# Two attention-and-FFN blocks on one core: all weight slots 192 bytes above the split activations, modulo 256

## What is computed

```python
def first_block(x, ...):
    for i in range(2):
        h = rmsnorm(x, norm_g[i])
        y = fox_mixer(h, ...) if i % 2 == 0 else nsa_mixer(h, ...)
        x = x + y
    return rmsnorm(x, final_g)

def second_block(x, ...):
    for layer in range(2):
        h = _rmsnorm(x, norm_mix[layer])
        y = _hgrn2_mixer(h, ...) if layer % 2 == 0 else _mla_mixer(h, ...)
        x = x + y
        x = x + _conv_ffn(_rmsnorm(x, norm_ffn[layer]), ...)   # 1024 -> 2 x 2816 -> 1024
    return x
```

## Time and profile before

| | |
|---|---|
| median of 3 runs | 1044.48 us (1043.44 to 1045.8) |
| profiled execution | 1047.28 us, its span 1045.5 us |
| TensorE (PE) busy | 1015.4 us, 97% |
| weight loads (PEld) busy | 967.8 us, 93% |
| VectorE (DVE) busy | 767.1 us, 73% |
| ScalarE (ACT) busy | 549.9 us, 53% |
| GpSimd (POOL) busy | 67.8 us, 6% |
| matmuls | 8176 |
| moved by DMA | 153.08 MB, 146 GB/s on average |

### The profile page before, as it was taken

One profiled execution on the slowest core, in us unless ns is written; L12 is line 12 of the kernel. 1 busy time (PEld: TensorE's weight loads), 2 busy tenths in 40 slices (PEclk: granted clock), 3 DMA queues, 4 the chain that ended last, 5 costly groups with the idle time before them and its releaser, 6 DMA issues. The chain is left out here.

```text
span 1045.5 us, 20361 instructions
## 1 busy us (share of the span) xinstructions
PE 1015.4 (97%) x8176; PEld 967.8 (93%) x8178; DVE 767.1 (73%) x1300; ACT 549.9 (53%) x869; POOL 67.8 (6%) x54
## 2 busy tenths in 40 slices
PE   7999999999999999999999999999999999999997
PEld 5998999998778999899999999999997899999997
DVE  4765775867787667497658878787867659878785
ACT  4644545364665656543555554545675455454541
POOL 3100005000000400000030000000001420000000
PEclk8999999999999999999999999999999999999999
DMA  8544444793112556401455656575531446665641
GB/s 275 168 123 133 138 134 142 236 283 96 66 42 82 163 172 202 149 1 34 129 162 161 203 160 201 162 202 159 147 121 42 121 127 197 180 200 169 198 136 41
DMA packets 184142, 153.08 MB, mean 146 GB/s; under 512 B 12478, under 2 KB 176901, under 8 KB 184069
## 3 DMA queue, kind: packets, MB, share of 16 engines
q1 hardware_dynamic: 183858, 152.01, 48.4%
q10 hardware_dynamic: 210, 0.05, 0.0%
HBM read 148.91 MB, written 1.05 MB: 143 GB/s over the span
## 5 line engine op out<-in xcount | busy, mean ns | idle before, releaser
L447 PE MATMUL bank<-h_high,w_high 128*128 128x256 f32 x1312 | 378.3, 288 | 6.7 <-DVE ffn_normed L1096 2.6
L449 PE MATMUL bank<-h_high,w_low 128*128 128x256 f32 x1312 | 371.6, 283 | 0.0
L448 PE MATMUL bank<-h_low,w_high 128*128 128x256 f32 x1312 | 371.5, 283 | 0.0
L399 ACT ACTIVATE w_high<-ring 128x2048 fp32r<-128x2048 f32 x137 | 261.5, 1912 | 160.3 <-PE bank L449 155.7
L409 DVE TENSOR_TENSOR w_low<-ring,w_high 128x2048 fp32r<-128x2048 f32 x118 | 271.3, 2300 | 32.9 <-ACT w_high L399 32.4
L447 PEld LDWEIGHTS bank<-h_high,w_high 128*128 128x128 f32 x1312 | 251.8, 192 | 9.2 <-issue 5.6
L448 PEld LDWEIGHTS bank<-h_low,w_high 128*128 128x128 f32 x1312 | 252.0, 192 | 0.5 <-issue 0.5
L449 PEld LDWEIGHTS bank<-h_high,w_low 128*128 128x128 f32 x1312 | 251.8, 192 | 0.0
L447 PE MATMUL bank<-ffn_hidden_high,w_high 128*128 (+1 forms) x352 | 99.7, 283 | 2.0 <-DVE ffn_hidden_low L1129 2.0
L448 PE MATMUL bank<-ffn_hidden_low,w_high 128*128 (+1 forms) x352 | 99.6, 283 | 0.0
L449 PE MATMUL bank<-ffn_hidden_high,w_low 128*128 (+1 forms) x352 | 99.6, 283 | 0.0
(11 more groups left out here) (352 smaller groups left out, 1752.5 us busy)
## 6 DMA issues: line engine op xcount, KB each, us to landing
ring<-in_ffn_w_up_dram SPq DMA_DIRECT2D x44, 1024.0 KB, 6.0
ring<-in_ffn_w_down_dram SPq DMA_DIRECT2D x22, 1024.0 KB, 5.0
ring<-in_fox_w_in_dram SPq DMA_DIRECT2D x16, 1024.0 KB, 5.8
ring<-in_hgrn_w_in_dram SPq DMA_DIRECT2D x16, 1024.0 KB, 5.5
ring<-in_nsa_w_in_dram SPq DMA_DIRECT2D x14, 1024.0 KB, 5.5
ring<-in_fox_w_out_dram SPq DMA_DIRECT2D x4, 1024.0 KB, 4.9
ring<-in_nsa_w_out_dram SPq DMA_DIRECT2D x4, 1024.0 KB, 5.0
ring<-in_hgrn_w_out_dram SPq DMA_DIRECT2D x4, 1024.0 KB, 5.0
```

Source lines behind the costliest of these rows:

```text
L399: i = nc.scalar.activation(dst, src, ACT.Copy)
L447: nc.tensor.matmul(o, ah, bh, start=start, stop=False, **kw)
L448: nc.tensor.matmul(o, ah, bl, start=False, stop=False, **kw)
L449: return nc.tensor.matmul(o, al, bh, start=False, stop=stop, **kw)
```

## The change

Six small buffers (eps, scratch, rstd, rstd_half, rstd_inner, gain_hgrn) are declared ahead of w_high instead of behind the constants, and the work area gets 13 columns more. Nothing else of the program differs.

```diff
         h_hi, h_lo = sb("h_high", [P, DC, S], F32R), sb("h_low", [P, DC, S], F32R)
+        eps, scratch = sb("eps", [P, 1]), sb("scratch", [P, 1])
+        rstd, rstd_half, rstd_in = [sb(n, [P, TT]) for n in ("rstd", "rstd_half", "rstd_inner")]
+        gain_hgrn = sb("gain_hgrn", [P, DC])
         w_hi, w_lo = sb("w_high", [P, NSLOT, SLOT], F32R), sb("w_low", [P, NSLOT, SLOT], F32R)
         ring = sb("ring", [P, NSLOT, SLOT])
         ncst = at["levels"][0]
@@
         pick_bf, cmask_bf = sb("pick_bf", [P, FOX_H], BF16), sb("cmask_bf", [P, TT * CMP], BF16)
-        eps, scratch = sb("eps", [P, 1]), sb("scratch", [P, 1])
-        rstd, rstd_half, rstd_in = [sb(n, [P, TT]) for n in ("rstd", "rstd_half", "rstd_inner")]
         row = sb("rstd_row", [P, S])
         w_f, b_f = sb("w_f", [P, DC, FOX_H]), sb("b_f", [P, FOX_H])
-        gain_hgrn = sb("gain_hgrn", [P, DC])
         lower_exp, lower, lower_rest = [sb(n, [P, DC]) for n in ("lower_exp", "lower", "lower_rest")]
         row2 = row[:, :].unsqueeze(1).broadcast_to([P, 2, S])
-        WORK = 23 * 1024 - 144 - S - DC * FOX_H - FOX_H - DC - 2 * TT - 1 - 4 * DC
+        WORK = 23 * 1024 - 131 - S - DC * FOX_H - FOX_H - DC - 2 * TT - 1 - 4 * DC
```

## The result

The changed kernel takes 1032.14 us (median of 4 runs, 1030.04 to 1033.06), the kernel before in the same comparison 1045.14 us. The ratio is 0.9875, 95% interval 0.9854 to 0.9895: 13.0 us faster. The profiled execution took 1032.14 us, its span is 1030.4 us. (The two profiled spans lie 15.1 us apart, 2 us more than the medians, because the profiled execution of the kernel before, 1047.28 us, was above its median.)

What follows compares the result with a forecast made beforehand. TensorE's step from matmul to matmul, nearly all in product3's triples, was taken as the bound. Terms summed to -13.9 us: profiled 1047.28 to 1033.4, less 2.8 for the median gives 1030.6 us, range 1006 to 1047.

Steps and rivals of the forecast that it cites:

- What bounds the kernel: TensorE, busy 97% of the span, sets the end; the step between matmul starts in product3's triples counts.
- Term 1: Weights stationary against h, ffn_hidden, hgrn_out and mla_out: distance 0 to 192, 5376 matmuls from 0.1200 to 0.1175 us, -12.9 us.
- The middle between two neighbours: Step of 0.1175 us taken for both new distances, 192 and 64, between 0.1164 and 0.1183.
- The ends 0.1164 and 0.1183: Steps seen at distances 224 and 32, taken as bounds for 192; the weights-stationary gain would be -18.6 or -8.8 us.
- Term 2: Weights moving against h, distance 0 to 64: 480 matmuls each 2.5 ns quicker, -1.2 us.
- Terms 3 and 4: Weights stationary against fox_out, blocks, lora, 32 to 192: -0.4 us; weights moving against blocks, 224 to 64: +0.1 us.
- Term 5: levels moving against hgrn_out, distance 32 to 0: 64 matmuls of 512 columns each 8 ns slower, +0.5 us.
- Term 6: Other readers of the constants and the shifted rstd_row and w_f: within 0.5 us either way, taken as 0.
- The reading that the distance acts: Stationary start minus moving start, modulo 256, sets the matmul step, not the place of one operand.
- The steady state stays at 0.1200: Rival: matmul and load settle into a fixed pattern at 192 too; +1.7 us, 1046.2 us; chance 0.14.
- The single long steps before the rotation: Steps at distance 192 before L1745, taken as 0.123 us; behind the slower rival, 1050 to 1065 us, chance 0.16.
- Much faster: Rival: the two reads hardly meet any more; mean step 0.1132 us, -42 us, 1005 us after some waits; chance 0.12.

Runs made afterwards that it cites:

- fine stream: Computation left out, quiet chip: runs of 32 matmuls at operand distances in steps of 4 bytes, three entries each; 118.2 to 118.9 ns at 72, 113.3 to 113.4 at 76.
- first stream: Computation left out: 48 matmuls per distance, 0 to 248 bytes in steps of 8, quiet, then beside VectorE and ScalarE; 120.0 ns at 0, 117.8 at 192.
- w0: Changed kernel with none of the small buffers ahead of the weights, only the longer work area left: 1044.76 us, ratio 0.9996 to the kernel before.
- moved64: Changed kernel with a 64-byte buffer ahead of x, everything 64 bytes further, distance still 192: 1029.78 us, ratio 0.9848 to the kernel before.
- the streams: Kernels without the computation: TensorE runs matmuls of one shape in a row while the distance between both operands changes; steps from 113.2 to 123.3 ns.
- w76: Changed kernel with split weights placed at distance 76 when stationary, 180 when moving: 1014.05 us, ratio 0.9699 to the kernel before.
- w88: Changed kernel with split weights placed at distance 88 when stationary, 168 when moving: 1016.28 us, ratio 0.9748 to the kernel before.
- w168: Changed kernel with split weights as views of one buffer, distance 168 when stationary, 88 when moving: 1040.81 us, ratio 0.9951 to the kernel before.
- w64: Changed kernel with two small buffers ahead of the weights instead of six, distance 64 stationary, 192 moving: 1022.21 us, ratio 0.9775 to the kernel before.
- w180: Changed kernel with split weights placed at distance 180 when stationary, 76 when moving: 1027.03 us, ratio 0.9799 to the kernel before.
- last stream: Computation left out, quiet: seven distances, each entered 16 times behind a small matmul of 40 to 100 columns, at two bases; 192 at 117.7 to 117.8 ns throughout.

## Why the prediction was right, and where it was not

The forecast was 1030.6 us in a range from 1006 to 1047, with 0.70 for faster; measured were 1032.14 us. The sum was -13.9 us, the medians moved by 13.0. The terms measured below come to -14.3 us, from one profile of each kernel; that lies inside the interval of the medians (11.0 to 15.3 us).

- **What bounds the kernel.** Right. All of the gain is in the steps of the triples, and it went through to the end: 231.1 and 231.0 us for everything else.
- **Term 1, weights stationary.** -12.9 was forecast. h went from 119.84 to 117.67 ns in 3832 steps (-8.3 us), ffn_hidden from 119.97 to 117.59 in 1051 (-2.5), hgrn_out and mla_out by some 2.1 in 379 (-0.8): -11.6 us. The middle between two neighbours, 0.1175, was 0.1 to 0.3 ns off. That it was so near is partly luck: the fine stream jumps by 5 ns between 72 and 76, so a neighbour 32 bytes away bounds nothing. The ends 0.1164 and 0.1183 were no bounds. The entry took part as well: 88 of the 92 unbroken runs of at least 20 steps at distance 192 ended near 117.8, and four near 113.5.
- **Term 2, weights moving.** -1.2 was forecast, -2.4 measured (444 steps, 119.90 to 114.54 ns). The step was mis-sized: for long stretches it is the quick pattern, which no run of triples had shown before.
- **Terms 3 and 4.** -0.4 and +0.1 forecast. fox_out and blocks 118.3 to 117.77 in 381 steps and lora 118.2 to 117.9 in 135 make -0.25; blocks stationary stayed (116.85 to 116.83), 0. Its 0.1164 in the prediction came from one stretch of 33 steps; all 96 average 0.1168. Distance 64 gave 114.54 against h and 116.83 against blocks in one and the same kernel, so here too the distance alone does not set the step.
- **Term 5, levels.** +0.5 forecast, 0 measured; the sign was a guess by analogy and wrong. 512 columns at distance 0 do not cost twice 0.1200. Mean steps are 232.3 before and 231.3 ns after, 1 ns in 47 steps. The first stream shows the same direction, 226.7 ns at distance 0 and 233.3 at 32 over the last 12 of 24 matmuls with 512 columns.

- **Term 6 and VectorE.** Right: 231.0 us for the other matmuls; between 590 and 690 us VectorE is busy for 80.49 us, where 81% was forecast from the earlier trace rows.

- **The reading that the distance acts.** Shown, for weights stationary, as the cause of the 0.1200 and of the gain: w0, moved64 and the streams leave neither the place of one operand nor the other engines for it. Incomplete, since the entry matters at many distances, and in part untested for weights moving.
- **The rivals.** "The steady state stays at 0.1200" named the right mechanism, a settled pattern, and asked the right question of 192. The answer is that 192 settles too, nearly always at 0.1178 (280/280/280 ns). The prediction expected it to roam there, and that sentence was wrong. The single long steps before the rotation said nothing about the mean, as the text suspected. "Much faster" came true for the weights moving, and for the weights stationary in w76 and w88.
- **The Trainium skill's rule** ("TensorE: Matmul & The Clock Gate", "Step-by-step: what each phase is for"), that loading the next weights does not steal read bandwidth from the running matmul, is not borne out here for float32r, since by it the distance could not matter. In a stream with nothing else running, 113.3 or 120.0 ns hang on where the two operands stand and on the entry. That the two reads collide is the nearest reading of it; no run took the weight load away, so it is argued and not shown.

## What to carry to other kernels

Where a stream of short float32r matmuls bounds a kernel, the two operands of TensorE must be looked at as a pair: their distance modulo 256 was worth 1.2% here by the change and 3% by w76, at no cost but some bytes of padding. Durations that are all alike are the sign of a settled pattern, and their size tells which: 276 ns in the quick one, 279 to 283 in the slower ones here. A slower one asks for a scan of distances; the scan needs several entries for each distance, since a distance that is quick once may be slow the next time, and it needs the starts that the kernel has for the moving operand. Take the distance that is quick in every entry (76), not one that was quick only in some (168), and then time the whole kernel: even 76 met entries there that made it slow. 52 was quick in its three entries too and was not tried in a kernel.

## What was new of the hardware

- A step of 256 float32r columns with fresh weights each time settles between 113.3 and 123.3 ns at a granted clock of 1.00. Many distances show one of 113.3 ns (272 cycles of 2.4 GHz), 116.7 (280), 117.8, 118.3 (284) and 120.0 (288), others lie between, such as 115.5 at 8 and 119.2 at 40. The quickest is 16 cycles above the number of columns.
- The pattern hangs on 4 bytes of distance (118.2 to 118.9 at 72, 113.3 at 76) and at many distances on the entry (168: 8 of 16 quick at either base).
- A pattern that is entered lasts: w168 ran its first FFN at 0.1134 and its second at 0.1200 us. It would explain why kernels with such distances vary from execution to execution, w64 by 1% and w180 by 1.2%, while w76 varies by 0.35%. With one profile of each this is not shown, and moved64, at a distance that had one value in all 32 entries of the last stream, varies by 0.7%.
- VectorE streaming beside TensorE did not change the step at 0, 8, 32, 88, 168 and 192, nor did ScalarE at 0, 8 and 168.
